# Half the inner products in the SSD output stage, exponents two chunks ahead, and half of w_out prepared beside it

## The chip, the cores and the metric

One Trainium2 chip, one core. The metric is the device time of one execution in microseconds (us). Five engines matter: TensorE (PE in the profile, PEld for its weight loads), VectorE (DVE), ScalarE (ACT), GpSimd (POOL) and the queue of SyncE (SP), which issues most transfers.

## What is computed

The reference is a two-block sequence model over 2048 tokens of width 1024. The change concerns the first block, where a state-space scan (SSD) runs in both directions over chunks of 128 tokens, and the output projection behind it:

```
xd   = x * dt
seg  = acum[:, None] - acum[None, :];  decay = exp(where(lower, seg, -inf))
cb   = C B^T                           (per group of 4 heads)
y_diag = sum_s cb[l,s] * decay[l,s,h] * xd[s,h,:]
y_off  = C h_start * exp(acum)
y      = y_forward + flip(y_backward) + d_skip * x
out    = concat(y_pool, rmsnorm(y * silu(z))) @ w_out
```

There are 16 chunks (NC), 16 heads of width 64, 4 groups and 2 directions. All matrices are float32. The states at the chunk borders of the backward direction were computed in the stage before and lie in DRAM; the forward state is carried here.

## The kernel before

The kernel is a sequence of stages; the change touches three of them.

**The front stage** (`front`, lines up to 728) projects the input, and near its end makes the small rows for the scan: the step sizes `dt` (softplus), the exponentials of the cumulated decays `xr`, `wst`, `cdec` on ACT, and stores them as `ssd_rows` for the next stage (lines 270 to 283).

**The SSD output stage** (`ssd_outputs`, lines 730 to 991) runs over the 16 chunks, two per turn of a hardware loop. For a chunk c the parts are:

- `early` (L924): two groups of matrix products, `psCB` = C B^T (L931, four products of 128x128) and `psS`, the sum that advances the forward state (L937, four products of 128x256). `front` of DVE (L867) copies `psCB` to `cb`, and updates the state `hf` (L874, L878).
- `exponents` (L945): eight times a pair of products (L951 with 10 rows, L952 with the mask) fills `psE` with the exponents of 4 heads of one direction, and ACT turns it into `dec` with one exponential of 128x512 (L856). `psE` is one buffer: the next pair waits for the exponential before it. The eight pairs for chunk c+1 stand between the inner products of chunk c (`beside`, L954).
- `products` of DVE (L884) multiplies `dec` by `cb`, one instruction of 128x2048 for each direction.
- `inside` (L955): for each half q of the heads, the product of the identity with `xk` = d_skip * x (L956), and then for each head and each direction one product of `dec` with `xd` (L962, 128x64). `xd` = x * dt is made by POOL for each direction (L829), `xk` by POOL as well (L835).
- `offset` (L940): C times the state, four products of 128x256 into `psO`, once with the forward state `hf` and once with the backward state `hb`. DVE scales and adds them: `forward` (L890, L892) and `backward` (L896, L900), and multiplies by the gate `zt` (L902). SP then stores `y` (L797).

The trace shows a float32 product as two instructions of PE. So one chunk has 64 instructions of L962, 8 each of L931 and L937, 16 of L942, 4 of L956, and one instruction for each of the 16 products of L951 and L952, whose operands are of the rounded type F32R.

The order on PE within a chunk is written out in `body` (L966): inner products of heads 0 to 7; `offset` with `hf`; `early` for chunk c+1; inner products of heads 8 to 15; a wait for DVE's L892; `offset` with `hb`. POOL's order is `xw` (L824), `xd` for direction 0, `xd` for direction 1 (after the last exponents pair of this chunk), the loads of the next exponent rows (L816, L818), and `xk`, which waits until L892 has read the `psY` of the chunk before. PE needs both `xd` and `xk` at the start of a chunk.

**The mixing stage** (`mix_out`, lines 1020 to 1324) begins with the preparation of `w_out`. For each of its 16 pieces SP loads it (L1056), DVE multiplies it by the gate row (L1154), ACT makes the high part `w_hi` (L1098), and DVE the low part `w_lo` (L1162). DVE's two instructions of neighbouring pieces alternate. SP waits until all 16 low parts are made before it loads the first token tile (L1057, then `load` of L1058), and only then can PE begin (L1237).

## Time and profile before

| | |
|---|---|
| median of 3 runs | 3810.97 us (3808.97 to 3817.95) |
| the profiled execution | 3810.99 us |
| its span in the profile | 3809.3 us |
| mean granted TensorE clock | 0.919 of full speed |
| PE busy | 3393.4 us (89% of the span) |
| DVE / ACT / POOL busy | 1673.0 / 881.7 / 325.0 us |

The page's second part cuts the span into 40 slices of 95.2 us; a digit is the busy share of an engine in tenths, or the clock that TensorE was granted in tenths of full speed. The SSD output stage begins at 1244.7 us of the span and ends at 1771.2 us, and PE's first product of the mixing stage stands at 1823 us. In the chain and the waits an engine's idle time is put down to what ended it. In a timeline, neighbouring instructions of one form are merged: the second number is the time from the first's start to the last's end, and ends of PE instructions are modelled, so the distance between starts says more than the duration.

### The profile page before, as it was taken

The page shows a single profiled execution, that of the slowest core. Times are in us where ns is not written, and L with a number is a line of the kernel's source. Part 1 is how long each engine was busy: PE and PEld are TensorE (multiplying, and loading weights), DVE is VectorE, ACT ScalarE, POOL GpSimd, SP SyncE. Part 2 cuts the span into 40 slices and gives each one's busy share as a digit, 9 for nine tenths or more (in the row PEclk, how much of TensorE's full clock was granted, in tenths as well). Part 3 has the DMA queues.
Part 4 walks back from the last instruction along what each step waited for, and adds up shares of the span by engine and source line. Part 5 has one row for each costly group of instructions (what it writes and reads, how often), then busy time and mean ns, then how long its engine had stood idle before and what let it go on. Part 6 is the DMA issues. An engine that isn't in the chain of part 4 may idle for free. (4 is left out here: it accounts for less than half of the span.)

```text
span 3809.3 us, 39306 instructions
## 1 busy us (share of the span) xinstructions
PE 3393.4 (89%) x15500; PEld 2672.1 (70%) x15500; DVE 1673.0 (44%) x1934; ACT 881.7 (23%) x1386; POOL 325.0 (9%) x229
## 2 busy tenths in 40 slices
PE   7899999979999699984799989999996999994876
PEld 7788888768877466663688867888775555552655
DVE  3744533671142255455444434333333655552444
ACT  2422121112111111111222222232321243435000
POOL 0100000000020233331000000000000000000111
PEclk9999999989999678786899999999998799997888
DMA  4222323332263422224333323222223221302121
GB/s 157 74 65 73 105 83 130 127 105 84 95 208 104 120 93 93 93 93 136 110 116 116 116 95 136 89 87 91 83 67 96 51 56 28 100 7 77 61 77 66
DMA packets 210811, 358.63 MB, mean 94 GB/s; under 512 B 21796, under 2 KB 143268, under 8 KB 202801
## 3 DMA queue, kind: packets, MB, share of 16 engines
q1 hardware_dynamic: 198694, 334.30, 27.2%
q10 hardware_dynamic: 4608, 16.78, 1.2%
q0 software_dynamic: 7392, 5.89, 0.8%
q8 instruction: 86, 1.41, 0.1%
q14 instruction: 31, 0.25, 0.0%
HBM read 235.03 MB, written 121.74 MB: 94 GB/s over the span
## 5 line engine op out<-in xcount | busy, mean ns | idle before, releaser
L632 PE MATMUL p_ps<-hmT_hi,p_w_hi 128*128 128x512 f32 x1312 | 526.1, 401 | 22.8 <-ACT p_work L355 17.2
L632 PE MATMUL p_ps<-hmT_hi,p_w_lo 128*128 128x512 f32 x1312 | 514.5, 392 | 0.0
L632 PE MATMUL p_ps<-hmT_lo,p_w_hi 128*128 128x512 f32 x1312 | 514.2, 392 | 0.0
L1682 PE MATMUL p_ps<-h2T_hi,p_w_hi 128*128 128x512 f32 x800 | 328.0, 410 | 19.3 <-DVE h2T_lo L1544 19.3
L1682 PE MATMUL p_ps<-h2T_hi,p_w_lo 128*128 128x512 f32 x800 | 315.6, 395 | 0.0
L1682 PE MATMUL p_ps<-h2T_lo,p_w_hi 128*128 128x512 f32 x800 | 315.3, 394 | 0.0
L632 PEld LDWEIGHTS p_ps<-hmT_hi,p_w_hi 128*128 128x128 f32 x1312 | 248.8, 190 | 77.1 <-issue 22.5
L632 PEld LDWEIGHTS p_ps<-hmT_hi,p_w_lo 128*128 128x128 f32 x1312 | 248.4, 189 | 53.5
L632 PEld LDWEIGHTS p_ps<-hmT_lo,p_w_hi 128*128 128x128 f32 x1312 | 249.0, 190 | 49.5
L1821 PE MATMUL t_psO<-t_prob,t_v 128*65 128x512 f32 (+3 forms) x640 | 261.1, 530 | 1.0 <-DVE t_out_turned L1919 0.2
L1876 ACT ACTIVATE t_prob<-t_psS 128x1024 f32<-128x1024 f32 (+1 forms) x160 | 150.2, 938 | 320.0 <-PE t_psS L1809 184.5
L1908 DVE TENSOR_REDUCE t_chunk_max<-t_psM 128x1 f32<-128x512 f32 (+2 forms) x320 | 182.2, 607 | 95.1 <-PE t_psM L1792 69.9
L1263 PE MATMUL psMix<-wo_hi,m_y_hi 128*128 128x512 f32 x512 | 201.6, 394 | 3.5 <-DVE m_y_lo L1178 3.5
L1263 PE MATMUL psMix<-wo_lo,m_y_hi 128*128 128x512 f32 x512 | 200.0, 391 | 0.0
L1263 PE MATMUL psMix<-wo_hi,m_y_lo 128*128 128x512 f32 x512 | 200.0, 391 | 0.0
L1682 PEld LDWEIGHTS p_ps<-h2T_hi,p_w_hi 128*128 128x128 f32 x800 | 152.8, 191 | 56.1 <-issue 24.7
L460 DVE COPY p_work<-p_ps 128x512 f32<-128x512 f32 (+3 forms) x97 | 58.3, 633 | 300.8 <-PE p_ps L652 261.6
L962 PEld LDWEIGHTS psY<-y_xd,y_decay 128*128 128x128 f32 x1024 | 170.6, 230 | 27.9 <-issue 20.6
L1682 PEld LDWEIGHTS p_ps<-h2T_lo,p_w_hi 128*128 128x128 f32 x800 | 152.7, 191 | 36.7 <-issue 6.0
L1682 PEld LDWEIGHTS p_ps<-h2T_hi,p_w_lo 128*128 128x128 f32 x800 | 152.4, 190 | 32.9
L856 ACT ACTIVATE y_decay<-psSeg 128x512 f32<-128x512 f32 x128 | 76.5, 597 | 421.6 <-PE psSeg L952 421.6
L962 PE MATMUL psY<-y_xd,y_decay 128*128 128x64 f32 x1024 | 158.8, 304 | 0.0
(343 smaller groups left out, 5571.8 us busy)
## 6 DMA issues: line engine op xcount, KB each, us to landing
p_w_raw<-in_w_in SPq DMA_DIRECT2D x66, 512.0 KB, 5.8
p_spare<-in_wada ACTq DMA_DIRECT2D x32, 512.0 KB, 5.0
p_spare<-scratch_xs_tok SPq DMA_DIRECT2D x19, 512.0 KB, 4.5
scratch_xs_tok<-p_work SPq DMA_DIRECT2D x8, 1152.0 KB, 6.2
p_work<-in_wada SPq DMA_DIRECT2D x16, 512.0 KB, 3.7
p_work<-in_x SPq DMA_DIRECT2D x16, 512.0 KB, 3.6
scratch_dT<-p_work SPq DMA_DIRECT2D x8, 1024.0 KB, 5.9
scratch_zpT<-p_work SPq DMA_DIRECT2D x8, 1024.0 KB, 4.0
```

What stands on the lines that cost most here:

```text
L460: v.tensor_copy(tok[:, 4 * g:4 * g + cnt, 0:width], tiles(PS[:, bank, :])[:, 0:cnt, 0:width]).then_inc(S["group_read"], 1)
L632: mm = pe.matmul(PS[:, c, 0:width], wt[n][:, q, :], xx[:, q, cols], start=(q == 0 and j == 0), stop=(q == KT - 1 and j == 2))
L856: act.activation(dec[n][:, 4 * q:4 * q + 4, :], psE[:], ACT.Exp).then_inc(S["exp_ok"], 1)
L962: mm = pe.matmul(psY[:, h * HD:(h + 1) * HD], dec[n][:, d * HEADS + h, :], xd[n][:, d, h * HD:(h + 1) * HD], start=False, stop=(h == 8 * q ...
L1263: mm = pe.matmul(psM[:, h, :], y[n][:, q, :], w[:, q, h * CH:(h + 1) * CH], start=(q == 0 and j == 0), stop=(q == MT - 1 and j == 2))
L1682: mm = pe.matmul(ps[:, c, :], wt[n][:, q, :], xx[:, q, c * CH:(c + 1) * CH], start=(q == 0 and j == 0), stop=(q == KT - 1 and j == 2))
L1821: mm = pe.matmul(psO[:, o:CH], va[n][:, kt + e, 0:VD], pt[p % 2][:, e, o:CH], start=(kt + e == 0), stop=(kt + e == 4 * qc + 3), skip_group ...
L1876: act.activation(pt[p % 2][:, :, off:CH], psS[p % 2][:, :, off:CH], ACT.Exp, scale=1.0 / 8).then_inc(S["prob"], 1)
L1908: v.reduce_max(mx[:, j, c:c + 1], psM[:, m % 2, 0:w], axis=AX_X).then_inc(S["first_read"], 1)
```

## The change

In the SSD output stage:

- The front stage stores ln(max(dt, 1e-37)) in place of dt. ACT adds it as a bias in the exponential, so `dec` already holds the step sizes and `xd` goes; the bias differs by head, so each exponential of 128x512 becomes four of 128x128.
- The decays of the two directions (`dec_f`, `dec_b`) are added by DVE before the one multiplication by `cb`, and each head has one inner product, with `xs` itself.
- `psE` has two buffers; its second is also `psCB`, which ACT copies now. Exponents run two chunks ahead, with three buffers for `dec_f`.
- PE's order is new: all inner products of a chunk stand together, and after them `offset` with `hb`, `sums` (L937 before) and, for two chunks ahead, `products` (L931 before), and `offset` with `hf`.
- POOL gates `y` in place of DVE; `y` has two buffers. The hardware loops are written out.
- Beside every second chunk one piece of `w_out` is prepared: POOL multiplies by the gate row, ACT makes the high and DVE the low part. The mixing stage prepares the other eight.

```diff
-                        sp.wait_ge(S["exp"], 4)
-                        sp.dma_start(a["ssd_rows"][0], dt).then_inc(S["dec_out"], 16)
+                        sp.wait_ge(S["exp"], 5)
+                        sp.dma_start(a["ssd_rows"][0], t1).then_inc(S["dec_out"], 16)
...
+                        act.activation(t1, t1, ACT.Ln).then_inc(S["exp"], 1)
...
+                    v.tensor_scalar(t1, dt, 1e-37, None, ALU.max)
...
-                    v.wait_ge(S["exp"], 5)
+                    v.wait_ge(S["exp"], 6)
...
+EARLY = 8
+def ssd(nc, kit, a, s, w):
+    NC = LT
...
+        dec_f, dec_b = some("y_decay_f", 3, [P, HEADS, P]), sb("y_decay_b", [P, HEADS, P])
...
+        piece = sb("y_w_piece", [P, D])
+        psE = kit.psum(ctx, "psSeg", [P, 2, 4, P])
+        psCB = psE[:, 1]
...
+                for c in range(NC):
+                    if c + 3 < NC:
+                        sp.wait_ge(S["cb"], c + 2)
+                        load_bT(c + 3)
+                        if c >= 1:
+                            sp.wait_ge(S["off_b"], c)
+                        load_cT(c + 3)
+                    if c + 2 < NC - 1:
+                        sp.wait_ge(S["summed"], c + 1)
+                        load_bt(c + 2)
+                    if c % 2 == 0:
+                        if c >= 2:
+                            sp.wait_ge(S["w_lo"], c // 2)
+                        sp.dma_start(piece[:], a["w_out"][:, c // 2, :]).then_inc(S["w_in"], 16)
+                    if c >= 1:
+                        sp.wait_ge(S["gated"], c)
+                        sp.dma_start(tokens(a["g_tok"], c - 1), y[(c - 1) % 2][:]).then_inc(y_out[(c - 1) % 2], 16)
+                    sp.dma_start(zt[:], tokens(a["z_tok"], c)).then_inc(S["z_in"], 16)
+                    if c + 2 < NC:
+                        sp.wait_ge(S["inside"], c + 1)
+                        load_xs(c + 2)
+                    if c + 2 < NC:
+                        sp.wait_ge(S["off_b"], c + 1)
+                        load_hb(c + 2)
...
+                for c in range(NC):
+                    if c + 1 < NC - 1:
+                        weighted(c + 1)
+                    if c >= 1:
+                        gated(c - 1)
+                    if c % 2 == 1:
+                        g.wait_ge(S["w_in"], 16 * (c // 2 + 1))
+                        g.tensor_tensor(piece[:], piece[:], w.gate[:], ALU.mult).then_inc(S["w_gated"], 1)
+                    if c + 1 < NC:
+                        skip(c + 1)
+                    if c + 3 < NC:
+                        g.wait_ge(S["seg"], 8 * (c + 3))
+                        load_rows(c + 3)
+                gated(NC - 1)
...
+                def copied(c):
+                    act.wait_ge(S["cb"], c + 1)
+                    if c >= 2:
+                        act.wait_ge(S["decays"], c - 1)
+                    act.activation(cb[c % 2][:], psCB, ACT.Copy).then_inc(S["cb_copied"], 1)
+                def exponentials(c):
+                    for q in range(8):
+                        act.wait_ge(S["seg"], 8 * c + q + 1)
+                        if q == 0 and c >= 3:
+                            act.wait_ge(S["inside"], c - 2)
+                        if q == 4 and c >= 1:
+                            act.wait_ge(S["merged"], c)
+                        out = dec_f[c % 3] if q < 4 else dec_b
+                        for j in range(4):
+                            h = 4 * q + j
+                            ins = act.activation(out[:, h % HEADS, :], psE[:, q % 2, j, :], ACT.Exp, bias=lndt[:, c, h:h + 1])
+                        ins.then_inc(S["exp"], 1)
+                act.wait_ge(S["rows_in"], 112)
...
+                def decays(c):
+                    v.wait_ge(S["exp"], 8 * c + 8)
+                    v.tensor_tensor(dec_f[c % 3][:], dec_f[c % 3][:], dec_b[:], ALU.add).then_inc(S["merged"], 1)
+                    v.wait_ge(S["merged"], c + 1)
+                    v.wait_ge(S["cb_copied"], c + 1)
+                    m = dec_f[c % 3][:].rearrange("p (g q) l -> p g q l", g=GROUPS)
+                    v.tensor_tensor(m, m, cb[c % 2][:].unsqueeze(2).to_broadcast([P, GROUPS, HPG, P]),
+                                    ALU.mult).then_inc(S["decays"], 1)
...
+                for c in range(NC):
+                    if c < NC - 1:
+                        state(c)
+                        decays(c + 1)
+                    forward(c)
+                    backward(c)
+                    if c % 2 == 1:
+                        q = c // 2
+                        v.wait_ge(S["w_hi"], q + 1)
+                        v.scalar_tensor_tensor(w.lo[:, q, :], piece[:], s.cols1[:, V_PSCALE + q:V_PSCALE + q + 1],
+                                               w.hi[:, q, :].bitcast(F32), ALU.mult, ALU.subtract).then_inc(S["w_lo"], 1)
...
+                def exponents(c, q):
+                    if q == 0:
+                        pe.wait_ge(S["seg_in"], 48 * (c + 1))
+                    if q == 1:
+                        pe.wait_ge(S["cb_copied"], c + 1)
+                    elif 8 * c + q >= 2:
+                        pe.wait_ge(S["exp"], 8 * c + q - 1)
...
+                def inside(c, heads):
+                    for h in heads:
+                        mm = pe.matmul(psY[:, h * HD:(h + 1) * HD], dec_f[c % 3][:, h, :], xs[c % 2][:, h * HD:(h + 1) * HD],
+                                       start=False, stop=h % 8 == 7, skip_group_check=True)
...
+                for c in range(2):
+                    products(c)
+                    for q in range(8):
+                        exponents(c, q)
+                    if c == 0:
+                        sums(0)
+                pe.wait_ge(S["rows_in"], 112)
+                for c in range(NC):
+                    ahead = (lambda q: exponents(c + 2, q)) if c + 2 < NC else (lambda q: None)
+                    if c + 2 < NC:
+                        products(c + 2)
+                    if c >= 1:
+                        pe.wait_ge(S["state"], c)
+                        pe.wait_ge(S["off_b_read"], c)
+                    offset(c, hf[c % 2]).then_inc(S["off_f"], 1)
+                    pe.wait_ge(S["decays"], c + 1)
+                    pe.wait_ge(S["skip"], c + 1)
+                    if c >= 1:
+                        pe.wait_ge(S["forward"], c)
+                    skipped(0)
+                    inside(c, range(0, 4))
+                    ahead(0)
+                    inside(c, range(4, 6))
+                    ahead(1)
+                    inside(c, range(6, 8))
+                    ahead(2)
+                    skipped(1)
+                    ahead(3)
...
+                    inside(c, range(14, 16)).then_inc(S["inside"], 1)
+                    ahead(7)
+                    pe.wait_ge(S["off_f_read"], c + 1)
+                    pe.wait_ge(h_in[c % 2], 16 * (c // 2 + 1))
+                    offset(c, hb[c % 2]).then_inc(S["off_b"], 1)
+                    if c + 1 < NC - 1:
+                        sums(c + 1)
...
-                for q in range(MT):
-                    if q >= 4:
-                        sp.wait_ge(S["w_lo_ok"], q - 3)
+                for q in range(EARLY, MT):
+                    if q >= EARLY + 4:
+                        sp.wait_ge(S["w_lo_ok"], q - EARLY - 3)
                     sp.dma_start(piece[q % 4][:], a["w_out"][:, q, :]).then_inc(p_in[q % 4], 16)
-                sp.wait_ge(S["w_lo_ok"], MT)
+                sp.wait_ge(S["w_lo_ok"], MT - EARLY)
```

## Rows read from the trace of the kernel before

**Rows 1.** Page, granted TensorE clock in 40 slices of the span

```profile
PEclk9999999989999678786899999999998799997888
```

**Rows 2.** Busy time by stretch: PE, PEld, DVE, ACT, POOL, then clock, DMA share, GB/s

```profile
1244.70:1285.40 40.70, 15.79 (x32) 8.13 (x33) 10.17 (x7) 6.06 (x9) 12.53 (x13) 0.54 0.57 170
1285.40:1749.40 464.00, 421.57 (x1741) 320.75 (x1741) 231.78 (x148) 71.69 (x120) 163.19 (x102) 0.77 0.27 88
1749.40:1771.20 21.80, 13.52 (x84) 11.24 (x84) 9.50 (x8) 0.00 (x0) 0.00 (x0) 0.89 0.21 72
1771.20:1822.70 51.50, 0.00 (x0) 0.00 (x0) 37.73 (x32) 18.38 (x16) 0.00 (x0) 0.50 0.70 218
```

**Rows 3.** Waits from 1240 to 1836: us in total, times, longest

```profile
PE psY L956 <- POOL y_xskip L835: 24.6, 15, 6.0
...
PE psO L942 <- DVE y_out L892: 22.7, 16, 1.5
```

**Rows 4.** Timeline of PE, 1577 to 1583: start, us, instruction

```profile
1577.39 1.05 PE L931 MATMUL psCB<-y_cT,y_bT 128*128 128x128 f32 x8
1578.28 1.89 PE L937 MATMUL psSt<-y_xw,y_b 128*128 128x256 f32 x8
1580.01 1.02 PE L956 MATMUL psY<-y_xskip,ident 128*128 128x512 f32 x2
1580.87 0.55 PE L962 MATMUL psY<-y_xd,y_decay 128*128 128x64 f32 x4
1581.35 0.49 PE L951 MATMUL psSeg<-y_seg_r,y_seg_l 10*128 10x512 f32 x1
1581.77 0.50 PE L952 MATMUL psSeg<-y_masks_r,y_ident 128*128 128x512 f32 x1
1582.11 1.00 PE L962 MATMUL psY<-y_xd,y_decay 128*128 128x64 f32 x8
```

**Rows 5.** DMA issues: count, KB each, us to landing

```profile
gate_row_sb<-scratch_gate_rows SPq DMA_DIRECT2D x1, 512.0 KB, 3.7
...
y_seg_r<-scratch_acum_rows POOLq DMA_DIRECT2D x16, 32.0 KB, 2.2
```

**Rows 6.** Timeline of ACT in the mixing stage, four of 128x128

```profile
1990.12 1.50 ACT L1123 ACTIVATE m_h<-psH,mod 128x128 f32<-128x128 f32 x4
```

**Rows 7.** Groups of instructions, whole span: busy, mean ns, idle before

```profile
L856 ACT ACTIVATE y_decay<-psSeg 128x512 f32<-128x512 f32 x128 | 76.5, 597 | 421.6 <-PE psSeg L952 421.6
...
L1479 ACT ACTIVATE p_side<-p_psG,cols 128x512 f32<-128x512 f32 x32 | 22.0, 689 | 9.7 <-PE p_psG L1662 9.5
...
L884 DVE TENSOR_TENSOR y_decay<-y_decay,y_cb 128x2048 f32<-128x2048 f32 x32 | 78.6, 2457 | 12.7 <-ACT y_decay L856 12.7
```

**Rows 8.** Busy time by stretch, columns as in rows 2

```profile
1529.90:1531.90 2.00, 0.00 (x0) 0.00 (x0) 1.97 (x3) 0.00 (x0) 2.00 (x2) 1.00 0.59 146
1532.50:1549.60 17.10, 17.10 (x54) 13.25 (x53) 3.18 (x2) 2.39 (x4) 5.07 (x2) 0.50 0.41 144
1549.60:1559.60 10.00, 9.98 (x56) 7.73 (x55) 6.38 (x5) 2.17 (x4) 0.23 (x1) 1.00 0.00 0
1559.60:1566.70 7.10, 5.25 (x10) 3.36 (x11) 5.50 (x4) 0.23 (x1) 7.08 (x6) 0.52 0.16 38
```

**Rows 9.** Timeline of PE, one offset group within the 17.10 us stretch

```profile
1545.40 3.73 PE L942 MATMUL psO<-ssd_hf,y_cT 128*128 128x256 f32 x8
```

**Rows 10.** Timeline at the stage's start: last of 17 SP loads, two of PE

```profile
1257.51 0.43 SPq L805 DMA_DIRECT2D y_z<-scratch_z_tok  x1
...
1269.08 0.79 PE L951 MATMUL psSeg<-y_seg_r,y_seg_l 10*128 10x512 f32 x1 [0.69 <-ACT y_decay L856]
1269.80 0.80 PE L952 MATMUL psSeg<-y_masks_r,y_ident 128*128 128x512 f32 x1
```

**Rows 11.** Timeline of DVE, two low parts of w_out

```profile
1785.72 1.28 DVE L1162 SCALAR_TENSOR_TENSOR wo_lo<-m_zp,cols,wo_hi 128x1024 fp32r<-128x1024 f32 x1
...
1788.05 1.28 DVE L1162 SCALAR_TENSOR_TENSOR wo_lo<-m_g,cols,wo_hi 128x1024 fp32r<-128x1024 f32 x1
```

More of the change, by code:

```diff
@@ new lines, in ssd @@
+        psCB = psE[:, 1]
+        psS, psY, psO = (kit.psum(ctx, n, [P, W_HALF]) for n in ("psSt", "psY", "psO"))
+        k = kit
+        S = k.sems("y_", ("cb", "cb_copied", "weighted", "summed", "state", "seg", "exp", "skip",
+                          "merged", "decays", "inside", "off_f", "off_f_read", "forward", "off_b", "off_b_read", "summed_y",
+                          "gated", "const", "rows_in", "masks_in", "const_in", "seg_in", "z_in", "w_in", "w_gated", "w_hi",
+                          "w_lo"))
@@ L837, in _ @@
[L837 to L848 removed]
+                                     both[m].rearrange("o (q j) l -> j (o q) l", j=4)).then_inc(S["seg_in"], 16)
@@ L849, in _ @@
+                gated(NC - 1)
             @block.scalar
             def _(act):
-                def body(c, half, n):
-                    for q in range(8):
-                        act.wait_ge(S["seg_ok"], 8 * c + q + 1)
-                        if q == 0 and (not isinstance(c, int) or c > 1):
-                            act.wait_ge(S["yd_ok"], c - 1)
-                        act.activation(dec[n][:, 4 * q:4 * q + 4, :], psE[:], ACT.Exp).then_inc(S["exp_ok"], 1)
-                for n in range(2):
-                    body(n, 0, n)
@@ new lines, in _ @@
+                act.wait_ge(S["rows_in"], 112)
+                for c in range(2):
+                    copied(c)
+                    exponentials(c)
+                for c in range(NC):
+                    if c + 2 < NC:
+                        copied(c + 2)
+                        exponentials(c + 2)
+                    if c % 2 == 1:
+                        q = c // 2
+                        act.wait_ge(S["w_gated"], q + 1)
+                        act.activation(w.hi[:, q, :], piece[:], ACT.Copy,
+                                       scale=s.cols1[:, V_PSCALE + q:V_PSCALE + q + 1]).then_inc(S["w_hi"], 1)
@@ new lines, in forward @@
+                def forward(c):
+                    v.wait_ge(S["off_f"], c + 1)
+                    if c >= 2:
+                        v.wait_ge(y_out[c % 2], 16 * (c // 2))
+                    v.tensor_tensor(by_head(y[c % 2][:]), by_head(psO[:]), heads_of(part(eac, c, 0)),
+                                    ALU.mult).then_inc(S["off_f_read"], 1)
+                    v.wait_ge(S["off_f_read"], c + 1)
+                    v.wait_ge(S["inside"], c + 1)
+                    v.tensor_tensor(y[c % 2][:], y[c % 2][:], psY[:], ALU.add).then_inc(S["forward"], 1)
@@ L954, in _, with skipped @@
-                beside = (2, 4, 5, 7, 9, 11, 13, 15)
-                def inside(c, n, q, last):
+                def skipped(q):
                     pe.matmul(psY[:, q * CH:(q + 1) * CH], s.ident[:], xk[:, q * CH:(q + 1) * CH],
                               start=True, stop=False, skip_group_check=True)
-                    for h in range(8 * q, 8 * q + 8):
-                        if not last and h in beside:
-                            exponents(c + 1, beside.index(h))
-                        for d in range(2):
-                            mm = pe.matmul(psY[:, h * HD:(h + 1) * HD], dec[n][:, d * HEADS + h, :],
-                                           xd[n][:, d, h * HD:(h + 1) * HD], start=False,
-                                           stop=(h == 8 * q + 7 and d == 1), skip_group_check=True)
-                    return mm
```

398 lines of the change are left out of this document (155 added, 243 removed).

## The prediction

> **What bounds the kernel now.** I read the page's clock line first. In slices 14 to 19, which hold the SSD output stage, TensorE was granted 6 to 8 tenths of full speed, against 9 around them [rows 1]. Then the busy time by stretch [rows 2]. The stage has three parts: 40.7 us of start, 464.0 us for 15 chunks with exponents beside them (30.93 us each), and 21.8 us for the last chunk. In the middle part PE is busy 421.57 us, 28.10 per chunk; DVE is busy 231.78 us (15.5 per chunk), ACT 71.69 (4.8) and POOL 163.19 (10.9). So PE bounds it, with 2.83 us of idle per chunk. The waits say what that idle is: 24.6 us for `xk` from POOL and 22.7 us for DVE's read of `psY` [rows 3], 3 us per chunk together. Behind the stage PE does nothing for 51.5 us, in which DVE is busy 37.73: the preparation of `w_out` and the first loads [rows 2].
>
> **PE's work of a chunk at full clock**, from distances between starts [rows 4]: L931's group 0.89 us, L937's group 1.73, a half of `xk` 0.86, four instructions of L962 0.48, an exponents pair 0.76. An `offset` group has the form of L937 and is put at 1.73. Before: 0.89 + 3 x 1.73 + 2 x 0.86 + 8 x 0.76 + 16 x 0.48 = 21.6 us. The measured 28.10 is 1.30 times that, and the mean clock of 0.77 gives 1/0.77 = 1.30. So a chunk is 21.6 us of work, stretched to 28.1 by the clock, and 2.8 us of waits.
>
> **The change, part by part.** T is the distance of one chunk to the next afterwards.
>
> *Half the inner products.* 32 of 64 instructions of L962 go: 8 x 0.48 = 3.84 us. Left are 17.7 us.
>
> *PE's order.* The wait for L892 goes, because L937's and L931's groups now stand where PE would wait; `xk` has from the end of the inner products to the next `skipped`: 0.76 + 3 x 1.73 + 0.89 = 6.8 us for one POOL instruction. `xd` goes. I leave 0.5 us of 2.83. Late next are the exponent rows: POOL issues them behind `xk`, some 2.3 + 1.8 us after the inner products end, they land 2.2 us later [rows 5], and PE asks at 6.8 + 0.86 + 0.96 = 8.6 us; 2.3 us are to spare, and an upper bound is 1 us lost per chunk. The exponents of the next chunk but one wait for nothing else, as `psE` is double.
>
> *ACT.* 32 exponentials of 128x128 with a bias take the place of 8 of 597 ns. Four of 128x128 with scale and bias from memory take 1.50 us in all [rows 6]; one operand less is 689 - 597 = 0.09 us less each [rows 7], so about 1.13 us for four, 1.50 at worst, and not below 0.60, the single one. PE offers a quarter each 0.76 + 0.48 = 1.24 us at full clock. I take 1.13: hidden. At 1.50 PE would wait 0.26 us in 8 quarters, 2 us per chunk. ACT's sum is 8 x 1.13 + 0.6 for the copy of `psCB` + 0.6 for half a piece of `w_out`, 10.2 us of T.
> The Trainium skill (ScalarE: Activation LUTs, What ACT_TABLE_LOAD costs) gives 280 ns + 0.833 ns per element with one pointer operand and an overlap of 93 ns, which is 1.27 us for four. The sum would be the same by it, but PE and ACT would then be level.
>
> *DVE.* It gives up the copy (0.7) and the gating and gets half a low part (0.64); the addition of the decays has the size of a product it replaces, 2.46 us [rows 7]. It stays near 14 us, and PE asks for its results a stretch later. *POOL* loses two `xd`, gets the gating and half a gate product: 9 to 11 us. Nothing there while T is above 15. *SP* stands each second chunk at `w_lo`, with the store of `y`, `zt`, `xs` and `hb` queued behind; those are asked for a whole chunk later, so it costs 0. The front stage gets one DVE and one ACT instruction and up to two table loads beside PE's projection: 0, at most 4 us.
>
> *The clock.* This is what I can't count. Of T = 17.7 + 0.5 = 18.2 us at full clock, how much runs at 1.2 GHz? The trace has three things [rows 8]. PE stood 2.0 us for `xk`, and the following 17.1 us were granted 0.50, although PE was busy throughout, with the thin inner products and exponents; it ended behind the dense group of L942 [rows 9]. Then 10.0 us at 1.00, of which the last 7 are again inner products, PE busy 9.98; and then 7.1 us at 0.52. So a long stretch of inner products lets the clock fall, and the dense groups bring it back. In the new order they are one block (offset, sums, products, offset, `skipped`, 6.9 us), and the thin stretch is 10.7 us with `skipped(1)` in its middle. I expect one late fall per chunk like the last one, 7.1 us at half speed: 3.5 us lost. T = 18.2 + 3.5 = 21.7. Bounds: 18.2 with no fall; 17.7/0.77 + 0.5 = 23.5 with the old share; with the rows late and ACT at its bound besides, 26.5; all at 1.2 GHz 2 x 17.7 + 0.5 = 35.9.
>
> *The start.* ACT now waits for `rows_in`, whose last load is the 20th of SP. 17 were issued in 12.8 us, 0.8 each [rows 10]: issued at 1260, landed 3.7 us later [rows 5] or, in the crowd, 5: 1265. Then two chunks of exponents before the first inner product. A pair at the low clock takes 0.72 + 0.80 = 1.52 us [rows 10]: 16 x 1.52 = 24.3, and with one sums, two products and one offset at that clock (2 x 5.2 = 10.5) and two tails of ACT (3.4), inner products begin at 1303, 18 us later than the 1285.4 of before.
>
> *The end.* Two chunks have no exponents. The first is bound by DVE (update 2.4, decays 4.9, `forward` 2.4, `backward` 2.9: 13 us), and the last takes the 21.8 us of before [rows 2] less 3.84 for its inner products and 1.73 for the offset, which now stands ahead of them, and 0.8 more as POOL gates: 17 us. Together 30.
>
> The stage then ends at 1303 + 14 T + 30 = 1333 + 14 T.
>
> *w_out.* Two low parts are 1788.05 - 1785.72 = 2.33 us apart [rows 11], and PE can't start before the last: 8 x 2.33 = 18.6 us go. If their part beside the chunks weren't hidden it would cost at most (1.2 + 1.15 + 1.28) x 8 = 29 us; I count 0, as DVE and ACT have 7 us and more free per chunk.
>
> **The sum.** Against the profiled execution's 3811.0 us: 3811.0 - (1771.2 - 1333 - 14 T) - 18.6 = 3354.2 + 14 T. With T = 21.7: 3658 us. The median of the three runs is the same within 0.1 us (its span is 3809.3, the rest lies around it).
>
> **Rivals.**
> *The clock stays up.* For it: no wait is left that PE showed, and dense groups stand together. Against it: the fall after 10.0 us with PE busy 9.98. T = 18.2, 3609 us. The Trainium skill (TensorE: Matmul & The Clock Gate, HAM oscillation) has idle gaps as what throttles the clock, and by that rule this rival would be the outcome; the trace disagrees at the place just named. Chance 0.17.
> *The clock is down as often as before, or ACT and the exponent rows hold PE.* T = 23.5 to 26.5: 3683 to 3725 us. For it: the thin stretch is now in one piece. Chance 0.25.
> *The clock stays down for the whole stage.* The exponents and single inner products never let it rise: T = 35.9, 3857 us. It decides from T = (3811 - 3354.2)/14 = 32.6 on. Against it: each dense group of before raised it, and these are now longer. Chance 0.03.
> *The change doesn't do what it says for w_out:* SP or DVE reach the pieces late, the chunk waits, and what is saved behind is paid before: up to 29 us more, 3687 us. Chance 0.05, inside the range.
> The forecast, T from 20 to 23 (3634 to 3676), has 0.50.
>
> **How the numbers follow.** The likeliest case gives 3658. The range reaches down to the clock that stays up, 3607, and up to T = 25.4, 3710. Faster than by 0.3% (11 us, what a measurement of this kernel can tell) in all cases but the one that stays down and what I haven't thought of: faster 0.96, same 0.01, slower 0.03.
>
> **What would show it.** The distance of chunks (starts of the `psY` addition) near 21.7 us; a granted clock of 0.8 to 0.9 in the stage, with one fall in each chunk's inner products; no `xk` row in the waits; ACT's four exponentials in 1.1 to 1.3 us; first inner product near 1303; the time from the stage's end to PE's first product 33 us for 51.5. Wrong would be: a chunk distance above 24 with the clock near 0.9, which would be a wait that I don't see; ACT's idle ended by nothing while PE waits for it; or low parts of `w_out` that DVE waits for.

## The result, and the profile after

The changed kernel takes 3645.26 us (median of 4 runs, 3642.95 to 3659.66) against 3811.57 us beside it: a ratio of 0.9569, with a 95% interval of 0.9542 to 0.9597. The forecast was 3658 us with a range of 3607 to 3710. The profiled execution took 3642.95 us, 168.04 less than that of before.

The page after has PE at 90% of a shorter span and this clock line, against [rows 1]; the stage lies in slices 14 to 18:

```profile
PE 3271.6 (90%) x14980; PEld 2567.9 (71%) x14980; DVE 1653.4 (45%) x1893; ACT 962.5 (26%) x1788; POOL 333.1 (9%) x220
...
PEclk9999999999999778878999989999996999996888
```

Busy time by stretch, columns as in [rows 2]: the start, 14 chunks with exponents beside them, the last two chunks, and the preparation of w_out.

```profile
1243.40:1299.80 56.40, 33.36 (x73) 18.72 (x74) 12.30 (x8) 21.15 (x68) 13.46 (x14) 0.53 0.52 154
1299.80:1583.40 283.60, 283.57 (x1170) 207.86 (x1169) 214.44 (x116) 143.06 (x468) 155.83 (x87) 0.87 0.48 148
1583.40:1620.20 36.80, 18.12 (x97) 14.07 (x95) 21.96 (x14) 1.15 (x1) 14.08 (x5) 0.82 0.25 86
1620.20:1652.20 32.00, 0.00 (x0) 0.00 (x0) 18.98 (x16) 9.19 (x8) 0.00 (x0) 0.50 0.63 205
```

The middle stretch is the result: T = 283.60/14 = 20.26 us where a chunk took 30.93, and PE is busy for 283.57 of 283.60 us. The stage is 149.7 us shorter (526.5 to 376.8), and the time behind it 19.4 us (51.5 to 32.1). PE's waits from 1243 to 1600 hold nothing of [rows 3] any more; all but one lie at the start:

```profile
PE psSeg L968 <- DMA y_cT<-scratch_cT: 14.5, 1, 14.5
PE psSeg L977 <- ACT y_cb L879: 7.4, 1, 7.4
PE psO L992 <- DVE y_out L931: 7.0, 1, 7.0
PE psSeg L977 <- DMA y_seg_l<-scratch_acum_rows: 5.8, 1, 5.8
```

What is left above the 17.63 us of work is clock. The windows of three chunks in a row (61.4 us, a period with which the starts of the chunks repeat) show two falls of the granted clock to 0.50, with PE busy in every one of these microseconds:

```profile
1412.10:1418.90 6.80, 6.80 (x18) 5.15 (x18) 2.02 (x2) 3.49 (x10) 3.64 (x4) 0.50 0.30 87
1418.90:1449.60 30.70, 30.70 (x147) 22.45 (x146) 29.02 (x15) 15.79 (x54) 18.95 (x9) 1.00 0.61 191
1449.60:1459.80 10.20, 10.20 (x26) 7.68 (x27) 5.00 (x5) 4.74 (x15) 3.64 (x4) 0.50 0.28 70
1459.80:1473.50 13.70, 13.70 (x66) 9.77 (x65) 12.40 (x7) 7.26 (x25) 5.88 (x2) 1.00 0.62 203
```

17.0 of 61.4 us run at 1.2 GHz; the work in them would take 8.5 us at 2.4 GHz, so a fall costs 8.5/3 = 2.8 us per chunk, and the work is (44.4 + 8.5)/3 = 17.63 us. Both falls begin among the last inner products of a chunk, one or two quarters before they end, and last through `offset` with `hb` into `sums`: at 1414.45 that `offset` takes 3.61 us, where the one with `hf` has 1.89 at the full clock. So in these chunks the dense block is itself in part run at 1.2 GHz. One exponents quarter of PE at full clock (1.24 us from L977 to L977), ACT's four exponentials, and DVE's last low part with PE's first product of the mixing stage, each from its engine's timeline:

```profile
1425.74 0.49 PE L977 MATMUL psSeg<-y_seg_r,y_seg_l 10*128 10x512 f32 x1
1426.16 0.50 PE L979 MATMUL psSeg<-y_masks_r,y_ident 128*128 128x512 f32 x1
1426.50 0.55 PE L1000 MATMUL psY<-y_xs,y_decay_f 128*128 128x64 f32 x4
1426.98 0.49 PE L977 MATMUL psSeg<-y_seg_r,y_seg_l 10*128 10x512 f32 x1
...
1408.63 1.14 ACT L890 ACTIVATE y_decay_f<-psSeg,y_lndt 128x128 f32<-128x128 f32 x4 [0.57 <-PE psSeg L979]
...
1646.71 1.28 DVE L1207 SCALAR_TENSOR_TENSOR wo_lo<-m_x,cols,wo_hi 128x1024 fp32r<-128x1024 f32 x1
...
1652.34 0.98 PE L1282 MATMUL psPool<-m_d,pool_w_sb 128*128 128x128 f32 x3 [42.42 <-DMA m_d<-scratch_dT]
```

### The profile page after: what moved, and what is told of

Its sections match the earlier page's. It is cut to its first block and busy times, and to the rows that moved or that the text cites. A ratio compares the mean times of both kernels' runs of the same rounds, so it can differ in the third digit from the quotient of the medians.

```text
span 3641.0 us, 37882 instructions
## 1 busy us (share of the span) xinstructions
PE 3271.6 (90%) x14980; PEld 2567.9 (71%) x14980; DVE 1653.4 (45%) x1893; ACT 962.5 (26%) x1788; POOL 333.1 (9%) x220
## 5 line engine op out<-in xcount | busy, mean ns | idle before, releaser
L1727 PE MATMUL p_ps<-h2T_hi,p_w_hi 128*128 128x512 f32 x800 | 327.3, 409 | 19.3 <-DVE h2T_lo L1589 19.3
L461 DVE COPY p_work<-p_ps 128x512 f32<-128x512 f32 (+3 forms) x97 | 58.3, 633 | 300.4 <-PE p_ps L654 261.4
L1837 PE MATMUL t_psM<-t_KM,t_QB 66*128 66x512 f32 (+2 forms) x320 | 131.5, 479 | 30.7 <-DMA t_v<-scratch_va_tok 27.2
L1866 PEld LDWEIGHTS t_psO<-t_prob,t_v 128*65 128x65 f32 x640 | 83.4, 137 | 96.6 <-issue 80.8
L1853 PE MATMUL t_psS<-t_QA,t_KA 128*128 128x512 f32 (+1 forms) x320 | 146.5, 458 | 3.3 <-DMA t_QB<-t_max_lo 3.2
L1583 DVE TENSOR_TENSOR p_w_lo<-p_w_raw,p_w_hi 128x1024 fp32r<-128x1024 f32 x25 | 37.4, 1497 | 240.9 <-ACT p_w_hi L1486 240.9
L446 DVE TENSOR_TENSOR p_w_lo<-p_w_raw,p_w_hi 128x1024 fp32r<-128x1024 f32 x41 | 51.1, 1245 | 163.6 <-ACT p_w_hi L319 163.4
L2198 PE MATMUL o_psR<-o_w_hi,o_y_hi 128*128 128x512 f32 x128 | 63.0, 492 | 65.4 <-DVE o_x L2154 64.8
```

The costliest lines, as they stand in the source:

```text
L446: v.tensor_tensor(w_lo[b % 2][:], w_raw[b % 2][:], w_hi[b % 2][:].bitcast(F32), ALU.subtract).then_inc(S["w_lo"], 1)
L461: v.tensor_copy(tok[:, 4 * g:4 * g + cnt, 0:width], tiles(PS[:, bank, :])[:, 0:cnt, 0:width]).then_inc(S["group_read"], 1)
L1583: v.tensor_tensor(w_lo[b % 2][:], w_raw[b % 2][:], w_hi[b % 2][:].bitcast(F32), ALU.subtract).then_inc(S["w_lo"], 1)
L1727: mm = pe.matmul(ps[:, c, :], wt[n][:, q, :], xx[:, q, c * CH:(c + 1) * CH], start=(q == 0 and j == 0), stop=(q == KT - 1 and j == 2))
L1837: mm = pe.matmul(psM[:, m % 2, 0:w], QB[n][0:KM_ROWS, j * P:(j + 1) * P], KM[n][:, c * CH:c * CH + w], start=True, stop=not edge, skip_gro ...
L1853: pe.matmul(out, KA[n][:, ks], QA[n][:, qs], start=True, stop=False, skip_group_check=True)
```

## The experiments

Each kernel was timed in three rounds beside the kernel before. Two of them are compared by their ratios to it, where 0.001 is 3.8 us; the change itself, 0.0431, is 164 us by that. T, the distance of one chunk to the next, is read from the starts of DVE's addition of `psY` in the profiled execution. The other parts of the change (PE's order, the removed `xd`) were not taken back one at a time, so no run shows what each is worth.

**Twice the inner products.**

```diff
-                        mm = pe.matmul(psY[...], dec_f[...], xs[...], start=False, stop=h % 8 == 7, ...)
+                        for twice in range(2):
+                            mm = pe.matmul(psY[...], dec_f[...], xs[...], start=False, stop=twice == 1 and h % 8 == 7, ...)
```

> The changed kernel with each inner product (L1000) issued twice, so psY holds twice the sum inside the chunk, which changes the output; nothing else. Theory (PE's work divided by the granted clock is the time of a chunk): a chunk gets the 3.84 us of full-clock work back that the change took out. At the changed kernel's clock of 0.87 that is 4.4 us per chunk, T from 20.26 to 24.7 and 3645 + 16 x 4.4 = 3716 us; as the thin stretch gets longer, the clock may fall more, up to the old share of 0.77, which gives (17.63 + 3.84)/0.77 = 27.9 and 3760 us. Rival (the gain comes from the order and the removed waits, and halving the products only made idle time): T under 21 with PE idle gone or little moved, time under 3660 us.

3677.84 us, ratio 0.963 [0.9602, 0.9657]. In the profiled execution (3691.68 us, the longest of four; the shortest is 3659.54) T is (1624.41 - 1314.11)/13 = 23.87 against 20.36 over the same chunks of the changed kernel. In this execution halving the products is thus worth about 3.5 us per chunk. The ratio rose by 0.0061 only, 23 us, where 16 chunks would give 56 to 61, and the runs lie 32 us apart: the time is between the rival's bound of 3660 and the theory's 3716. In the profiled run a chunk lasts 21.37 us at a full clock and 24.5 to 29 us with a fall, and the clock stayed up for five chunks in a row (1463.88, 1485.25, ... 1570.75). The 21.37 us against 17.63 confirm the work, 3.74 us for 3.84. The mean granted clock of the whole execution was 0.939 in this one and 0.942 to 0.947 in the three shorter ones, against 0.931 to 0.937 in the four of the changed kernel: with more inner products the clock fell less, and a part of the added work came back by it. How many falls the shorter runs had can't be seen. The rival's T under 21 falls for the profiled run, and the fear that the clock would sink to 0.77 was wrong too.

**No w_out beside the chunks.** The four blocks for `piece` in the stage go, and the mixing stage's loops run from `FIRST`, which is 0. The cut shows the first block and one of the loops.

```diff
-                    if c % 2 == 0:
-                        if c >= 2:
-                            sp.wait_ge(S["w_lo"], c // 2)
-                        sp.dma_start(piece[:], a["w_out"][:, c // 2, :]).then_inc(S["w_in"], 16)
...
-                for q in range(EARLY, MT):
+                for q in range(FIRST, MT):
```

> The changed kernel without the preparation of w_out beside the chunks: the mixing stage prepares all 16 pieces, as the kernel before. Theory (hidden beside the chunks, 2.33 us each behind the stage): the chunk distance stays at 20.3 us, PE waits 51 us in place of 32 behind the stage, 3645 + 18.6 = 3664 us. Rival (the pieces are paid beside the chunks, as they take POOL and DVE): T falls below 19.5, the stage gets 8 to 15 us shorter, and the total is 3650 to 3656 us.

3658.09 us, ratio 0.9602 [0.9585, 0.9619], so the pieces are worth 0.0033, 13 us, though the two intervals overlap by 0.0012; they don't exclude the expected 18.6 us either. T stays at (1574.89 - 1310.01)/13 = 20.38: beside the 14 chunks they are free. From the last store of `y` to PE's first product it takes 55.4 us (1610.05 to 1665.47) where the changed kernel takes 36.5 (1615.87 to 1652.34), so 18.9 us are gained there. Without the pieces the last store is issued at 1610.05 and not at 1615.87. Of these 5.8 us, 4.8 lie in the end part: from the 14th addition of `psY` to the last store it takes 35.2 us (from 1574.89) for 39.9 (from 1575.94). There PE waits for DVE, and a piece lengthens DVE's path. The other microsecond lies ahead of the chunks, where the two executions are already 1.3 us apart at the first addition.

**One buffer's worth of overlap for the exponents.**

```diff
                     if q == 1:
                         pe.wait_ge(S["cb_copied"], c + 1)
-                    elif 8 * c + q >= 2:
-                        pe.wait_ge(S["exp"], 8 * c + q - 1)
+                    if 8 * c + q >= 1:
+                        pe.wait_ge(S["exp"], 8 * c + q)
```

> The changed kernel, in which each exponents pair waits for the exponentials of the pair just before it (exp >= 8c + q) in place of the one before that, so the second buffer of psE gives no overlap. Theory (the double buffer is a part of the gain, as ACT's four exponentials take 1.14 us and PE has only 0.48 us of inner products beside them): PE waits 0.5 to 0.8 us in six to eight quarters of a chunk, 4 to 6 us per chunk at full clock, T from 20.3 to 24 to 27 us, 3700 to 3740 us. Rival (at the low clock PE's quarter is long enough, and the waits fall where the clock would fall anyway): T under 21.5, under 3665 us.

3787.15 us, ratio 0.9938 [0.992, 0.9955]. The waits are a little under the expected 4 to 6 us per chunk, and time and T far above their ranges: of the 164 us that the whole change brings, 141 go when this overlap goes. T is (1691.57 - 1338.10)/12 = 29.46 us. Busy time over these 12 chunks, and two quarters of PE's timeline in them:

```profile
1338.10:1691.57 353.47, 309.42 (x1008) 214.26 (x1008) 191.24 (x103) 122.50 (x402) 140.67 (x78) 0.67 0.35 110
...
1506.34 0.79 PE L977 MATMUL psSeg<-y_seg_r,y_seg_l 10*128 10x512 f32 x1 [0.48 <-ACT y_decay_f L890]
1507.06 0.80 PE L979 MATMUL psSeg<-y_masks_r,y_ident 128*128 128x512 f32 x1
1507.66 0.95 PE L1000 MATMUL psY<-y_xs,y_decay_f 128*128 128x64 f32 x4
1509.09 0.79 PE L977 MATMUL psSeg<-y_seg_r,y_seg_l 10*128 10x512 f32 x1 [0.48 <-ACT y_decay_b L890]
```

The waits are 44.05/12 = 3.67 us per chunk, six of them and none over 0.9 us, and busy time rises from 20.26 to 25.8: short waits between products bring the clock from 0.87 to 0.67, and that costs more (5.5 us) than the waits.

**A dense group amid the thin stretch.**

```diff
                     ahead(6)
+                    if c + 1 < NC - 1:
+                        sums(c + 1)
...
                     offset(c, hb[c % 2]).then_inc(S["off_b"], 1)
-                    if c + 1 < NC - 1:
-                        sums(c + 1)
```

> The changed kernel with sums(c + 1) (8 dense products of 128x256, 1.73 us) moved from behind the offset with hb into the inner products, between heads 12 to 13 with their exponents and heads 14 to 15; same work, same output. Theory (a long stretch of single inner products and exponents lets the clock fall, and a dense group amid it prevents that): the granted clock of the 14 chunks rises from 0.87 to 0.92 or more, T from 20.26 to 19.2 or less, 3630 us or less. Rival 1 (the clock goes by the whole work of a chunk, wherever it stands): T and clock unchanged within 0.3 us, 3640 to 3650 us. Rival 2 (PE now waits there for xw or the state): a wait of some us per chunk in PE's row of L985, slower than 3650 us.

3684.32 us, ratio 0.9653 [0.9627, 0.9679]: 32 us slower than the changed kernel, and no expectation met. From 1337.13 to 1571.51 a chunk takes 23.44 us at a clock of 0.80:

```profile
1337.13:1571.51 234.38, 224.06 (x841) 161.29 (x841) 157.37 (x86) 102.37 (x335) 110.99 (x65) 0.80 0.45 138
```

PE's waits are 1.0 us per chunk, for the exponent rows and `psO` (none for `xw` or the state), and the rest is clock. The dense group amid the thin stretch didn't keep the clock up. Why it fell further is not shown: the move took `sums` out of the block, and it also brought the waits, one of 0.5 us for `psO` in each chunk, and the run above has short waits alone lower the clock.

**128 rows for the exponent product.** The operands of L977 (L980 in this kernel) get 118 rows of zeros; the 512 columns, the number of instructions and the result stay.

```diff
-        seg_r, seg_l = sb("y_seg_r", [10, NDH * P], F32R), sb("y_seg_l", [10, 8, P], F32R)
+        seg_r, seg_l = sb("y_seg_r", [P, NDH * P], F32R), sb("y_seg_l", [P, 8, P], F32R)
...
-                g.dma_start(seg_r[:], a["seg_r"]).then_inc(S["const_in"], 16)
-                g.dma_start(seg_l[:], a["seg_l"]).then_inc(S["const_in"], 16)
+                g.wait_ge(S["zero"], 2)
+                g.dma_start(seg_r[0:10], a["seg_r"]).then_inc(S["const_in"], 16)
+                g.dma_start(seg_l[0:10], a["seg_l"]).then_inc(S["const_in"], 16)
...
+                v.memset(seg_r[:].bitcast(F32), 0.0).then_inc(S["zero"], 1)
+                v.memset(seg_l[:].bitcast(F32), 0.0).then_inc(S["zero"], 1)
```

> The changed kernel with the operands of the first exponent product (seg_l, seg_r, 10 rows) filled up to 128 rows with zeros, once at the start by DVE; same output, same count and shape of columns. Theory (the 10-row products count as little work for the clock gate, and that is why the clock falls while PE is busy throughout): the clock stays at 1.00 in the 14 chunks, T = 17.7 us, 3645 - 14 x 2.6 + some 3 us of zeroing = 3612 us. Rival (the rows in use make no difference to the clock; the thin inner products alone let it fall): T 20.3 and clock 0.87, 3645 to 3650 us.

3603.5 us, ratio 0.9458 [0.9442, 0.9475], 42 us faster than the changed kernel, in place of the 33 expected, and the way there is another. T is (1539.65 - 1322.39)/12 = 18.1 at a clock of 0.96, busy 16.55 and idle 1.55. A quarter at full clock in PE's timeline:

```profile
1322.39:1539.65 217.26, 198.66 (x1008) 161.88 (x1008) 198.28 (x102) 117.58 (x408) 142.48 (x79) 0.96 0.57 176
...
1439.39 0.48 PE L980 MATMUL psSeg<-y_seg_r,y_seg_l 128*128 128x512 f32 x1
1439.71 0.39 PE L982 MATMUL psSeg<-y_masks_r,y_ident 128*128 128x512 f32 x1
1439.94 0.55 PE L1003 MATMUL psY<-y_xs,y_decay_f 128*128 128x64 f32 x4
1440.43 0.50 PE L980 MATMUL psSeg<-y_seg_r,y_seg_l 128*128 128x512 f32 x1
```

From L980 to L1003 it is 0.55 us where it was 0.76 with ten rows, and a quarter takes 0.91 us (from 1438.48) or 1.04 (from 1439.39) where it took 1.24. So the zeros do two things: PE's work shrinks, and the clock stays up. DVE and ACT are now next to bound: from 1300 to 1560 PE waits 17.7 us for L932's read of `psO`, 7.9 for ACT and 1.2 for the exponent rows.

**The zeros with the doubled products** separate work from clock, since here PE hardly waits.

> The version with zeros (3603.5 us, T = 18.1) with each inner product issued twice, so psY holds twice the sum inside the chunk. Theory (at a clock that stays up, the halving is worth its 3.84 us of work, less what lies in PE's waits of 1.55 us per chunk): T from 18.1 to 20.4 to 21.9, 3640 to 3660 us; without the zeros the same doubling gave 32.6 us only, as it brought the clock from 0.87 to 0.89. Rival (at the full clock DVE bounds the chunk): T under 19.5, under 3628 us.

3619.35 us, ratio 0.9491 [0.9466, 0.9516]; T = (1553.00 - 1325.35)/12 = 18.97 at a clock of 1.00. The rival's numbers hold, but not its reason: PE is busy 225.24 of 227.65 us, so it isn't DVE that bounds the chunk. Without the doubling DVE, ACT and a few falls kept the chunk at 18.1 us, so with the zeros in place the halving is worth 0.9 us of T, and 0.0033 or 13 us of time.

```profile
1325.35:1553.00 227.65, 225.24 (x1393) 197.12 (x1392) 197.94 (x102) 122.87 (x403) 138.24 (x78) 1.00 0.56 167
...
1454.42 0.47 PE L980 MATMUL psSeg<-y_seg_r,y_seg_l 128*128 128x512 f32 x1
1454.73 0.39 PE L982 MATMUL psSeg<-y_masks_r,y_ident 128*128 128x512 f32 x1
1454.96 1.00 PE L1004 MATMUL psY<-y_xs,y_decay_f 128*128 128x64 f32 x8
1455.77 0.48 PE L980 MATMUL psSeg<-y_seg_r,y_seg_l 128*128 128x512 f32 x1
```

Here the same quarter of doubled products takes 1.35 us (1454.42 to 1455.77); without the zeros, also at 1.00, it takes 1.69 (1495.35 to 1497.04) in PE's timeline of the run of doubled products:

```profile
1495.35 1.00 PE L1001 MATMUL psY<-y_xs,y_decay_f 128*128 128x64 f32 x8
1496.28 0.49 PE L977 MATMUL psSeg<-y_seg_r,y_seg_l 10*128 10x512 f32 x1
1496.70 0.50 PE L979 MATMUL psSeg<-y_masks_r,y_ident 128*128 128x512 f32 x1
1497.04 1.00 PE L1001 MATMUL psY<-y_xs,y_decay_f 128*128 128x64 f32 x8
```

So a ten-row product among products of 128 rows costs 0.34 us of PE, 2.7 us per chunk: 17.63 us of work become some 15 by this estimate, and with the 3.84 us of doubled products that is 18.8, against 18.97 measured.

**The same zeros in the kernel before.** The same edit of L736, L837 and L838 and two zeroings by DVE.

> The kernel before with the same zeros below the ten rows of seg_l and seg_r, and nothing else changed. Theory (the 10-row products let the clock fall in the kernel before as well): its 15 chunks run at a granted clock of 0.95 or more in place of 0.77, 30.9 us a chunk falls to 24.5 to 26, 3735 to 3720 us; the change's own part of the gain would then be some 120 us against this kernel. Rival (there the falls come from the waits for xk and L892, and from twice as many thin products): clock under 0.82, 3790 us or more.

3736.06 us, ratio 0.9805 [0.9785, 0.9825]: 74 us, 1 us short of the expected range. The clock isn't where it was expected, at 0.95 or more: T is 23.6 in most chunks and 29.5 in some, and the clock 0.89 for 0.77, so some falls stay, as its waits do (26.6 us for `xk`, 19.9 for the read of `psY`). Against this kernel the change is worth 90 us, where 120 were expected, and with the zeros in both, 132.

**Single overlap and zeros.**

> The version in which each exponents pair waits for the exponentials of the pair just before it, now with the zeros below the ten rows of seg_l and seg_r. Without the zeros it had T = 29.46 us: 3.67 us of PE idle and 25.8 us busy at a clock of 0.67. Theory (the single buffer costs mostly through the clock: short waits in the thin stretch let it fall): with the zeros the clock stays at 0.9 or more, the waits stay at 3.7 to 5 us, T = 16.5 + 4.5 = 21 us, 3640 to 3660 us. Rival (waits alone bring the clock down, whatever the products are): T of 26 or more, 3715 us or more.

3723.6 us, ratio 0.9762 [0.9737, 0.9787]. The time is the rival's, T lies between: (1658.83 - 1355.04)/12 = 25.3 us, 4.76 idle and 20.6 busy at a clock of 0.81.

```profile
1355.04:1658.83 303.79, 246.72 (x1008) 192.85 (x1008) 194.06 (x103) 123.52 (x405) 139.91 (x78) 0.81 0.40 125
```

So zeros don't protect from waits: six or seven of up to 0.9 us in a chunk bring the clock down by themselves, and the second buffer is worth 116 us here too.

**Three steps on top of the zeros.** First, DVE reads `psO` (L931) before the decays of the next chunk; `added` is the addition of `psY` (L935), cut off from `forward`:

```diff
                     if c < NC - 1:
                         state(c)
+                    forward(c)
+                    if c < NC - 1:
                         decays(c + 1)
-                    forward(c)
+                    added(c)
```

> The version with the exponent operands filled up to 128 rows with zeros (3603.5 us), and in DVE's order the read of psO (L931) stands ahead of the decays of the next chunk. Theory (with the clock up, PE waits behind the inner products for L931, 17.7 us in all, 7.0 of them in the last chunk but one): these waits go, T from 18.0 to 17.5 and the end part 6 us shorter, 3588 to 3596 us. Rival (DVE, at 16.3 of 18.0 us in each chunk, is itself the bound and the wait only moves to the merged decays or the next read of psY): within 3 us of 3603.

3602.67 us, ratio 0.9449 [0.943, 0.9468]: no change that can be told. The wait for `psO` is gone, and PE waits 15.1 us for ACT's L891, which waits 14.9 for the merged decays, since `dec_b` is one buffer. The rival's clause was right. Then, with that order, DVE gates `y` in POOL's place:

> As the version with DVE's read of psO first, and DVE gates y in place of POOL (one multiplication of 128x1024, SBUF operands). Theory (DVE's and POOL's instructions on SBUF lengthen each other, so POOL's 3.35 us gating costs DVE about as much as gating itself would): DVE's busy time per chunk stays at 16 to 16.6 us although it has one instruction of 1.3 us more; L914, L922 and L926 get shorter (3.1, 2.7 and 3.4 us); time within 5 us of the version without it, 3583 to 3598 us. Rival (no such coupling; DVE gets 1.3 us more per chunk and is the bound): T above 18.3, 3605 us or more.

3605.1 us, ratio 0.9454 [0.9438, 0.9471]: within 5 us of the version without it, as the theory has it, but outside its 3583 to 3598 us, which counted on a gain that the step before didn't bring. T is 218.43/12 = 18.2, just under the rival's 18.3. What decides is DVE's busy time. DVE has 12 gatings more over 12 chunks, and its busy time per chunk goes from 192.91/12 = 16.1 to 194.74/12 = 16.2 us. DVE's and POOL's groups over 12 chunks, POOL gating first, then DVE gating:

```profile
L841 POOL TENSOR_TENSOR y_out<-y_out,y_z 128x1024 f32<-128x1024 f32 x12 | 40.1, 3338 | 0.0
L922 DVE TENSOR_TENSOR y_decay_f<-y_decay_f,y_decay_b 128x2048 f32<-128x2048 f32 x12 | 39.4, 3280 | 0.0
L914 DVE TENSOR_TENSOR y_tmp<-y_hf,y_cdec 128x1024 f32<-128x1024 f32 x12 | 37.1, 3090 | 0.2
```

```profile
L940 DVE TENSOR_TENSOR y_out<-y_out,y_z 128x1024 f32<-128x1024 f32 x12 | 33.7, 2807 | 0.4
L907 DVE TENSOR_TENSOR y_tmp<-y_hf,y_cdec 128x1024 f32<-128x1024 f32 x12 | 27.5, 2294 | 0.0
L915 DVE TENSOR_TENSOR y_decay_f<-y_decay_f,y_decay_b 128x2048 f32<-128x2048 f32 x12 | 27.4, 2281 | 0.0
```

So a gating by POOL costs DVE about as much as gating itself. Last, the addition of the decays goes to the head of DVE's chunk (POOL gates again; `merged` is that addition with its wait, cut off from `decays`):

```diff
                     if c < NC - 1:
+                        merged(c + 1)
                         state(c)
```

> The version with zeros and DVE's read of psO first, and besides the addition of the two directions' decays (L921) for chunk c + 1 moved ahead of the state update. Theory (in the version it comes from, PE waits 1.2 us per chunk for ACT, which waits for that addition, as dec_b is single): both waits go, T from 17.9 to 16.8, 3585 to 3592 us. Rival (DVE, busy 16.1 of 17.9 us, is the bound, and the state or the decays come late instead): within 4 us of 3602.7.

3589.84 us, ratio 0.9405 [0.9381, 0.9429], inside the expected range: this is the fastest version, 0.983 of the changed kernel by the two ratios. T is 17.5 (209.54/12) in the profiled execution, the longest of the four (3598.45 us), and not the expected 16.8. The waits for ACT are down to 0.6 us. PE's largest wait is now that for the exponent rows, 11.6 us. With ACT released by the ln(dt) rows alone at the start:

> As the version with the addition first, and ACT waits at the start for the ln(dt) rows alone, not for the last of SP's 20 loads. Theory (PE's 7.4 us of idle behind psCB at the start is ACT waiting for rows_in): the first inner product comes 5 to 8 us earlier and the time falls by as much. Rival (the loads of cT and the exponent rows end PE's wait at the same time anyway): the same within 3 us.

3593.93 us, ratio 0.9425 [0.94, 0.9449]: the same. PE's first addition of `xk` comes 47.3 us (before this edit) and 47.5 us (with it) after its first product. As the rival has it, another thing ends the wait. In the timeline with this edit POOL issues the constants at 1247.4 and 1247.9, behind the zeroing of their tiles, is held until 1258.2 by their landing, and PE's first exponent product waits until 1267.3 for the rows.

```profile
1247.93 0.52 POOL L851 DMA_DIRECT2D y_seg_l<-in_seg_l  x1
1258.16 0.52 POOL L845 DMA_DIRECT2D y_seg_r<-scratch_acum_rows  x1 [9.71 <-DMA y_seg_l<-in_seg_l]
...
1267.31 0.80 PE L987 MATMUL psSeg<-y_seg_r,y_seg_l 128*128 128x512 f32 x1 [17.83 <-DMA y_seg_l<-scratch_acum_rows]
```

## Why the prediction held, and where it didn't

*Time.* 3658 forecast, 3645.26 measured (3642.95 in the profiled run): 13 us too long. With the measured T the formula 3354.2 + 14 T gives 3637.8; 6.8 us more for the end, 3.2 less for the first inner product (1299.8 for 1303) and 0.8 less behind the stage make 3640.6, so 2 us of the profiled run's 3642.95 lie elsewhere. The terms missed to both sides, 14 T by 20 us too long and the end by 7 too short, so the 13 us are in part luck.

*Work.* 17.7 us forecast, 17.63 measured. The doubled products confirm the part of the halving as work, 3.74 us for 3.84; as time it was worth 3.5 us per chunk in one execution and 23 us in all by the ratio.

*Waits.* 0.5 us of 2.83 was left; 0.0 is measured. Of the 10.67 us by which a chunk got shorter, 3.97 are work, 2.83 waits and 3.87 clock (30.93 - 21.6 - 2.8 = 6.5 before, 20.26 - 17.63 = 2.6 after).

*Clock.* The mis-sized term. I expected one late fall of 7.1 us per chunk, 3.5 us; there are two falls in three chunks, of 6.8 and 10.2 us, 2.8 us per chunk in these three and 2.6 over the 14. That falls come with PE busy throughout, and so not the clock that stays up, was right: by the idle-gap rule of the Trainium skill (TensorE: Matmul & The Clock Gate, HAM oscillation) no fall was due, and the windows of 6.80 and 10.20 us at 0.50 contradict it once more. It does hold in one direction: added waits brought the clock down (0.87 to 0.67). My picture behind the term was that a long thin stretch lets the clock fall and a dense group brings it back. It isn't borne out: a dense group amid the stretch went with 0.80 for 0.87, and the falls last through `offset` with `hb`. That the number came near is luck in so far.

*ACT.* 1.13 us for four exponentials, 1.14 measured. What I passed over in one clause ("as `psE` is double") is the largest single thing in the change: without that overlap 141 of its 164 us are gone, since 1.14 us of ACT beside 0.48 us of products makes six short waits per chunk, and these pull the clock down. The number didn't suffer, since with both buffers nothing is lost; but the prediction doesn't say that the gain hangs on them.

*DVE.* 14 us forecast, 214.44/14 = 15.3 measured: POOL's gating lengthens DVE's instructions. It cost nothing in the 14 chunks, where PE was busy throughout, but it is a part of the end.

*The end.* 30 us forecast, 36.8 measured. The last chunk took 17.5 us (1602.7 to 1620.2) for the 17 of the forecast; the last but one is where the sum was short. There PE stood 7.0 us for L931, behind L925. I had put 13 us for this chunk, DVE's instructions at undisturbed durations, and it took 19.3 (1583.4 to 1602.7). The timeline has L913 and L925 beside POOL's gating and `xk`:

```profile
1582.51 1.28 DVE L958 SCALAR_TENSOR_TENSOR wo_early_lo<-y_w_piece,cols,wo_early_hi 128x1024 fp32r<-128x1024 f32 x1
1582.67 3.33 POOL L841 TENSOR_TENSOR y_out<-y_out,y_z 128x1024 f32<-128x1024 f32 x1 [4.79 <-DVE y_out L942]
1583.70 3.37 DVE L913 TENSOR_TENSOR y_tmp<-y_hf,y_cdec 128x1024 f32<-128x1024 f32 x1
1587.11 1.22 DVE L917 TENSOR_TENSOR y_hf<-y_tmp,psSt 128x1024 f32<-128x1024 f32 x1
1588.36 2.29 DVE L921 TENSOR_TENSOR y_decay_f<-y_decay_f,y_decay_b 128x2048 f32<-128x2048 f32 x1
1588.90 3.51 POOL L837 TENSOR_TENSOR y_xskip<-y_xs,y_dskip 128x1024 f32<-128x1024 f32 x1 [2.91 <-PE psY L1000]
1590.69 3.87 DVE L925 TENSOR_TENSOR y_decay_f<-y_decay_f,y_cb 128x2048 f32<-128x2048 f32 x1
1594.48 1.21 DVE L931 TENSOR_TENSOR y_out<-psO,y_eac 128x1024 f32<-128x1024 f32 x1
```

*The start.* 58.3 us forecast (1244.7 to 1303), 56.4 measured. ACT did wait for the last load of `rows_in`, until 1266.71 where 1265 was forecast:

```profile
1266.71 0.60 ACT L879 ACTIVATE y_cb<-psSeg 128x512 f32<-128x512 f32 x1 [39.01 <-DMA gate_row_sb<-scratch_gate_rows]
```

That freeing ACT brought nothing was measured with the zeros, where the exponent rows land only then; the changed kernel itself has no such run. The front stage's added instructions cost nothing that can be seen: the stage begins at 1243.40, for 1244.70 before.

*w_out.* 18.6 us forecast behind the stage, 19.4 measured. "I count 0" for their part beside the chunks is right for the 14 chunks (T 20.36 and 20.38) and wrong for the end part, where it takes back 4.8 us; the rival of 29 us fell.

What stays open is what exactly the clock follows. Two things move it, in two pairs of kernels each: short waits bring it down (0.87 to 0.67, and 0.96 to 0.81 with the zeros), and 128 rows in place of ten bring it up (0.87 to 0.96, and 0.77 to 0.89 in the kernel before). Doubled products bring it up a little (0.88 for 0.86 over the same chunks, and in the mean of every execution). With the moved sums it was lower, but there waits came along. No run shows one rule behind them.

## What to carry to other kernels

Ask of each buffer that a change doubles what would happen to the clock without it, and not only how long the wait would be: here 3.7 us of short waits per chunk cost 9.2. Look for small-row products between full ones and try zeros in the unused rows, as filling them up with zeros was worth 42 us here and 74 us in the kernel before for two zeroings. Price DVE's work in a part where it bounds from its durations beside POOL, and price work moved "beside" something separately for the last turns, where the cover has run out.

## What was not expected of the hardware

- A product with 10 rows among products with 128 costs 0.34 us more per pair at a granted clock of 1.00 (1.69 against 1.35 us a quarter), although the columns are the same. The Trainium skill (TensorEngine Tiling (Array Packing), Key Properties) says that changing the tiling mode drains TensorE. By that rule a switch to a small-row mode and back would be paid twice per pair; that the ten-row product does run in another mode no row shows. The 0.34 us don't point to one place: the distance from the ten-row product to the mask's is 0.42 us and 0.31 with zeros, from there to the inner products 0.34 and 0.23, and on to the next ten-row product 0.93 and 0.81.
- DVE's instructions with two operands in SBUF take 2.29 us of 128x2048 alone and up to 4.35 beside POOL's in the changed kernel, and 1.2 to 3.4 us of 128x1024; POOL's gating takes 2.35 alone and 3.3 to 4.4 beside them. Those that read PSUM (L917, L931, L935, L938) stay at 1.21 to 1.23 us. The Trainium skill (SBUF — State Buffer, SBUF: two separate sides) has a port pair that such a DVE instruction and a GpSimd instruction can only hold one at a time. The trace agrees: in the timeline of the end, POOL's gating ends 2.2 us after L958 does (1586.00 and 1583.79), and L913 1.1 us after the gating (1587.07), near the 2.35 and 1.22 us that they take alone.
- Four exponentials of 128x128 with a bias pointer take 1.14 us, twelve without a gap 3.62 us, 0.30 each. The Trainium skill (ScalarE: Activation LUTs, What ACT_TABLE_LOAD costs), which the prediction weighed, has figures that give an estimate of 1.27 us for four; the measurement decides.
- Small loads issued by POOL took long to land in the crowd at the stage's start: in the kernel with ACT freed the constants held POOL for 9.7 us and their exponent rows PE until 7 us after the last issue, where 2.2 us is the middle value of the 16 such issues of the kernel before [rows 5].
